# Column halves around the layer norms of a hybrid encoder step, and memory attention cut into steps

## What is computed

```python
x = LN1(ALPHA * x + 0.5 * swiglu1(x))                 # FFN width 2816
proj = x @ w_mix_in                                   # conv input, q, k, v, index queries and keys
x = LN2(ALPHA * x + concat(conv(proj), topk_attention(proj)) @ w_mix_out)
x = LN3(ALPHA * x + mem_attention(x @ w_mem_q, mem_k, mem_v) @ w_mem_o)   # 4 heads, 256 memory rows
x = LN4(ALPHA * x + 0.5 * swiglu2(x))
```

## Time and profile before

| | |
|---|---|
| three runs | 2760.41, 2766.08, 2769.19 us, median 2766.08 |
| profiled execution | span 2761.0 us from first to last instruction; no other time is given for it |
| TensorE matmuls | busy 2571.3 us (93% of the span), mean granted clock 0.946 |
| VectorE, ScalarE, GpSimd | busy 1042.4, 968.6, 1324.2 us |
| HBM | 218.93 MB read, 21.87 MB written |

### The profile page before, as it was taken

How to read it: one execution, slowest core, us unless ns; L and a number is a source line. 1 busy time by engine, 2 the same in 40 slices (tenths; PEclk the granted TensorE clock), 3 DMA queues, 4 the chain that set the end, 5 groups by cost and what they waited for, 6 DMA issues and landing times.

```text
span 2761.0 us, 40053 instructions
## 1 busy us (share of the span) xinstructions
PE 2571.3 (93%) x15097; PEld 2214.4 (80%) x15097; DVE 1042.4 (38%) x1705; ACT 968.6 (35%) x1469; POOL 1324.2 (48%) x717
## 2 busy tenths in 40 slices
PE   7899999898799998997989989999999899899997
PEld 6899999898688886774489789999965676688885
DVE  3000001605573004237562488888335625200003
ACT  4432323323333333326523333232345242433332
POOL 1366666533366667540024246666620332566665
PEclk9999999899899999997689989999989899899998
DMA  6422332234233332335022123322230222333332
GB/s 187 144 84 84 92 92 70 77 87 165 62 99 96 95 89 75 90 99 157 9 62 92 43 66 91 92 86 85 81 132 1 62 61 61 92 99 101 113 98 73
DMA packets 420706, 244.39 MB, mean 89 GB/s; under 512 B 23857, under 2 KB 412017, under 8 KB 419185
## 3 DMA queue, kind: packets, MB, share of 16 engines
q1 hardware_dynamic: 389088, 195.65, 24.5%
q10 hardware_dynamic: 27520, 23.34, 2.8%
q0 software_dynamic: 3984, 23.86, 2.4%
HBM read 218.93 MB, written 21.87 MB: 87 GB/s over the span
## 4 chain that ended last, share of the span: by engine, by line
PE 76%; DVE 6%; POOL 6%; issue 5%; ACT 4%; DMA 2%; ACTq 1%; POOLq 0%; DVEq 0%; SPq 0%
PE LIN L506 64%; PE LIN L673 4%; POOL WL L1519 3%; PE TR L687 2%; PE TR L701 2%; DVE Y L1292 1%; PE LIN L769 1%; DVE Y L1318 1%; PE LIN L740 1%; POOL HL L1596 1%; POOL FP L1593 1%; PE LIN L656 1%; PE LIN L612 1%; DVE QSUM L1236 1%; DMA WRAW<-in_w_mem_v 1%
## 5 line engine op out<-in xcount | busy, mean ns | idle before, releaser
L1519 POOL TENSOR_TENSOR WL<-WRAW,WH 128x1024 fp32r<-128x1024 f32 x366 | 882.9, 2413 | 826.5 <-ACT WH L806 805.5
L506 PE MATMUL LIN<-XH,WH 128*128 128x272 f32 (+2 forms) x3048 | 833.7, 328 | 42.7 <-DVE XL L1287 18.2
L506 PE MATMUL LIN<-XL,WH 128*128 128x272 f32 (+2 forms) x3048 | 829.7, 327 | 0.0
L506 PE MATMUL LIN<-XH,WL 128*128 128x272 f32 (+2 forms) x3048 | 825.6, 325 | 0.0
L506 PEld LDWEIGHTS LIN<-XH,WH 128*128 128x128 f32 (+1 forms) x3048 | 515.2, 191 | 98.3 <-issue 43.6
L506 PEld LDWEIGHTS LIN<-XL,WH 128*128 128x128 f32 (+1 forms) x3048 | 517.4, 191 | 45.1 <-issue 0.2
L506 PEld LDWEIGHTS LIN<-XH,WL 128*128 128x128 f32 (+1 forms) x3048 | 515.3, 190 | 46.0 <-issue 0.4
L806 ACT ACTIVATE WH<-WRAW 128x1024 fp32r<-128x1024 f32 x382 | 402.1, 1053 | 229.3 <-PE LIN L506 130.3
L811 ACT ACTIVATE FG<-LIN 128x512 f32<-128x512 f32 (+1 forms) x272 | 166.7, 613 | 845.5 <-PE LIN L506 843.5
L506 PE MATMUL LIN<-HH,WH 128*128 128x272 f32 (+2 forms) x1376 | 376.5, 323 | 9.4 <-DVEq L1503 3.8
L506 PE MATMUL LIN<-HL,WH 128*128 128x272 f32 (+2 forms) x1376 | 374.1, 321 | 0.0
(11 more groups left out here) (184 smaller groups left out, 1922.1 us busy)
## 6 DMA issues: line engine op xcount, KB each, us to landing
WRAW<-in_ffn_gate SPq DMA_DIRECT2D x88, 512.0 KB, 3.8
WRAW<-in_ffn_up SPq DMA_DIRECT2D x88, 512.0 KB, 3.8
WRAW<-in_ffn_down SPq DMA_DIRECT2D x64, 512.0 KB, 4.1
WRAW<-in_w_mix_in SPq DMA_DIRECT2D x44, 512.0 KB, 3.8
WRAW<-in_ffn_down SPq DMA_DIRECT2D x32, 384.0 KB, 3.4
WRAW<-in_w_mix_out SPq DMA_DIRECT2D x16, 512.0 KB, 4.2
WRAW<-in_w_mem_q SPq DMA_DIRECT2D x16, 512.0 KB, 4.2
WRAW<-in_w_mem_o SPq DMA_DIRECT2D x16, 512.0 KB, 4.1
```

The costliest lines, as they stand in the source:

```text
L506: last = pe.matmul(LIN[0:outputs, slot, a, 0:g.width], wt[:, w, c, 0:outputs], x[:, c, a * g.width:(a + 1) * g.width], start=(c == 0 and w ...
L1519: pool.tensor_tensor(WL[:, n % RING, :, :], WRAW[:, n % 2, :, :], WH[:, n % RING, :, :].bitcast(F32), ALU.subtract).then_inc(lo_split, 1)
```

## The change

- The sample rows move from group 0 to group 1, so group 0 has 512 columns and group 1 has 544. Each group has two halves of columns, 256 and 256, or 256 and 288.
- The stages and their loops give way to an unrolled plan. A run of stages of a group between two attentions is one segment without barriers ("chain").
- In mixout, memq, memo, the last down part of each FFN, and the first four tiles of mix and of FFN 2, products are made for a half: four weight tiles for half 0, then the same four for half 1. A tile is given back when half 1 has used it; then the tile four further on is split. Other products take all columns.
- A norm is cut into twelve steps for each half. Half 0's are hung on the last four half-1 products, half 1's on the first four half-0 products of what follows, each step in the middle ("mid") or at the end of a product. An engine does the mid steps of a product, then its own work for that product, then the weight split, then the end steps; TensorE does mid steps ahead of chunk 4.
- The shift by chunk 0's mean is now a matmul in the product itself (LESS1, and PART1 for chunk 0). CSUM is added by GpSimd for chunks 1 to 6. ALPHA is taken in with the product's addition; only ahead of FFN 2 ScalarE still scales, all eight chunks in step 11.
- Down products of the last part are added to Y by VectorE out of PSUM, without ScalarE and GpSimd. FFN_PARTS is 6, 8, 8, and a split takes only the chunks that a tile has.
- Memory attention is cut into four units (half, pair of heads) of seven steps, hung on memq's and memo's products. Its value products use a part of LIN of their own.
- The stores of conv rows of both groups come in the index stage of group 1. The final norm of group 1's tiles 0 and 1 is hung on the last half-1 products.

The core of the diff (in it, the last three pieces are VectorE's sums, VectorE's norm steps and GpSimd's loop):

```diff
-MEAN_AT, POWER_AT = 0, 8
-FFN_PARTS = [(0, 8), (8, 8), (16, 6)]
+MEAN_AT, POWER_AT = 288, 296
+FFN_PARTS = [(0, 6), (6, 8), (14, 8)]
...
-        self.sample = index == 0
+        self.sample = index == 1
...
+        self.halves = [(0, 256), (256, self.cols - 256)]
+        self.half_tiles = [[0, 1], [2, 3] + ([4] if self.sample else [])]
...
+        while k < len(tiles):
+            halves = blocks(k)
+            size = min(RING, len(tiles) - k) if halves else 1
+            for half in (0, 1) if halves else (None,):
+                for i in range(size):
+                    src, j, more = tiles[k + i]
+                    pr = self.add(base + k + i, name, j, g, half, nk, src[2])
+                    pr.tell(**facts, **more)
+                    made.append(pr)
+            k += size
...
+    last = [pr for pr in made if pr.half == 1][-4:]
+    for h, four in ((0, last), (1, [pr for pr in following if pr.half == 0][:4])):
+        def at(i, where, *steps):
+            (four[i].mid if where == "mid" else four[i].end).extend([("norm", norm, h, s) for s in steps])
+        at(0, "mid", 0)
+        if four[0].pair:
+            at(1, "mid", 1)
+        else:
+            at(0, "end", 1)
+        at(1, "end", 2, 3)
+        at(2, "mid", 4, 5)
+        at(2, "end", 6)
+        at(3, "mid", 7, 8)
+        at(3, "end", 9, 10)
+        if alpha:
+            at(3, "end", 11)
...
+    where = [(p, w) for p in memq[5:] + memo[:4] for w in ("mid", "end")][1:]
+    starts = {(0, 0): 0, (1, 0): 6, (0, 1): 13, (1, 1): 21}
+    for (h, q), at in starts.items():
+        for step in range(7):
+            pr, w = where[at + step]
+            (pr.mid if w == "mid" else pr.end).append(("memory", h, q, step))
...
+                for pr in prs:
+                    if pr.first:
+                        pe.wait_ge(lo_split, pr.tile + 1)
+                    if pr.turn:
+                        pe.wait_ge(product_read[pr.slot], pr.turn)
...
+                    if lead.kind == "down" and lead.j == 0:
+                        pe.wait_ge(hidden_lo, PLAN.hidden_done[lead.which, lead.g.index, lead.part, c, lead.half])
+                    if lead.after_norm is not None and lead.pair:
+                        low_wait(pe, lead.half, lead.after_norm, c)
...
+                        if c == pr.nk - 1:
+                            if pr.norm is not None and pr.j:
+                                out, col, w = pr.parts[0]
+                                pe.wait_ge(shift_source[pr.half], pr.norm + 1)
+                                last = pe.matmul(LIN[:, pr.slot, out:out + w], LESS1[:, :], XH[:, 0, col:col + w],
+                                                 start=False, stop=True)
...
+                if pr.norm is not None and pr.j == 1:
+                    pe.wait_ge(shift_source[pr.half], pr.norm + 1)
+                    pe.matmul(spread(pr.half, pr.w), PART1[:, :], XH[:, 0, cols(pr)], start=True, stop=True)\
+                        .then_inc(shift_done[pr.half], 1)
+                for strand in pr.mid:
+                    take_up(strand)
...
+                h, y = pr.half, Y[:, pr.j, cols(pr)]
+                dve.wait_ge(product, pr.p + 1)
+                if pr.name == "ffn":
+                    last = dve.tensor_tensor(y, in_psum(pr), y, ALU.add)
+                else:
+                    last = dve.scalar_tensor_tensor(y, y, ALPHA, in_psum(pr), ALU.mult, ALU.add)
+                last.then_inc(product_read[pr.slot], 1)
+                dve.wait_ge(product_read[pr.slot], pr.turn + 1)
+                if pr.j == 1:
+                    dve.wait_ge(shift_done[h], pr.norm + 1)
+                    dve.tensor_tensor(Y[:, 0, cols(pr)], Y[:, 0, cols(pr)], spread(h, pr.w), ALU.subtract)\
+                        .then_inc(first_centred[h], 1)
+                if pr.j == KD - 1:
+                    dve.wait_ge(chunk_added[h], (KD - 2) * (pr.norm + 1))
+                    dve.tensor_tensor(CSUM[:, cols(pr)], CSUM[:, cols(pr)], y, ALU.add).then_inc(sum_done[h], 1)
+                if pr.j >= 2:
+                    add_square(pr, pr.j - 1)
+                if pr.j == KD - 1:
+                    add_square(pr, pr.j)
...
+                if 3 <= step <= 10:
+                    j = step - 3
+                    if j == 0:
+                        dve.wait_ge(inv_done[h], norm + 1)
+                    y = Y[:, j, c0:c0 + w]
+                    dve.wait_ge(dve_step, less[h, j])
+                    done = after(dve.scalar_tensor_tensor(y, y, GCOL[:, gain_of(norm), j:j + 1], spread(h, w),
+                                                          ALU.mult, ALU.mult))
+                    if j + 4 < KD:
+                        less_mean(j + 4)
+                    dve.wait_ge(dve_step, done)
+                    dve.tensor_scalar(y, y, BCOL[:, gain_of(norm), j:j + 1], None, ALU.add).then_inc(biased[h], 1)
+                    if j - 1 in DVE_LOW:
+                        low_part(j - 1)
+                    if j == KD - 1:
+                        low_part(j)
...
+                elif name == "chain":
+                    for prs in paired(products):
+                        if prs[0].name == "ffn" and prs[0].which == 2 and not g.sample and prs[0].part == 1 \
+                                and prs[0].kind == "down" and prs[0].j == 0:
+                            reload_queries(GROUPS[1])
+                        for pr in prs:
+                            for strand in pr.mid:
+                                take_up(strand)
+                        for pr in prs:
+                            if pr.norm is not None:
+                                statistics(pr)
+                            elif pr.name == "ffn":
+                                consume_ffn(pr)
+                        for pr in prs:
+                            if pr.last:
+                                split_lo(pr.tile + RING)
+                        for pr in prs:
+                            for strand in pr.end:
+                                take_up(strand)
```

More of the change, by code:

```diff
@@ L202, in load_tiles, with __init__, tell @@
                      for col, rows in g.tiles]
-def half(i, m):
-    return i * 2 + m // 2
+class Product:
+    def __init__(self, p, tile, name, j, g, half, nk, rows):
+        self.p, self.tile, self.name, self.j, self.g, self.half = p, tile, name, j, g, half
+        self.nk, self.rows = nk, rows
+        self.slot = p % 2
+        self.turn = p // 2
+        self.col, self.w = (0, g.cols if g else N_MEM) if half is None else g.halves[half]
+        if half is None and self.w > 512:
+            self.parts = [(256, 0, 256), (512, 256, self.w - 256)]
+        else:
+            self.parts = [(0, self.col, self.w)]
+        self.first = self.last = False
+        self.pair = False
+        self.mid, self.end = [], []
+        self.event = 0
+        self.tell()
+    def tell(self, which=0, after_norm=None, norm=None, kind="", f=0, part=0):
+        self.which, self.after_norm, self.norm = which, after_norm, norm
+        self.kind, self.f, self.part = kind, f, part
@@ new lines, in memory_strands, with pair_up @@
+def memory_strands(memq, memo):
+    where = [(p, w) for p in memq[5:] + memo[:4] for w in ("mid", "end")][1:]
[4 more added lines that the diff above has]
+            (pr.mid if w == "mid" else pr.end).append(("memory", h, q, step))
+def pair_up(made):
+    for half in (0, 1):
+        two = [pr for pr in made if pr.half == half][:2]
+        for pr in two:
+            pr.pair = True
@@ L429, in mean_of, with paired, memory_parts @@
-        def mean_of(g, slot):
-            return TR[:, slot, :].rearrange("p (a b) -> p a b", a=2)[:, 0:g.parts, 0:g.width]
+                engine.wait_ge(x_lo[h], len(POOL_LOW) * norm + POOL_LOW.index(j) + 1)
+        def paired(products):
+            out, k = [], 0
+            while k < len(products):
+                n = 2 if products[k].pair else 1
+                out.append(products[k:k + n])
+                k += n
+            return out
+        def memory_parts(g, h):
+            return [(i, *g.tiles[t]) for i, t in enumerate(g.half_tiles[h])]
@@ L478, in begin @@
                     pe.wait_ge(pool_end, s)
-            def norm_before(s):
-                return STAGES[s - 1]["norm"] if s and STAGES[s - 1]["name"] == "ln" and STAGES[s - 1]["which"] != 4 \
-                    else None
-            def column_mean(g, slot, matrix, src):
-                for a in range(g.parts):
-                    last = pe.matmul(TR[:, slot, 512 * a:512 * a + g.width], matrix[:, :],
-                                     src[:, a * g.width:(a + 1) * g.width], start=True, stop=True)
-                return last
@@ new lines, in take_up, with prs_of_queries @@
+            def take_up(strand):
+                kind, *what = strand
+                if kind == "norm":
+                    norm_step(*what)
+                elif kind == "memory":
+                    memory_step(current[0], *what)
```

(21 more changed lines are left out.)

1826 lines of the change are left out of this document (924 added, 902 removed).

## The result

The changed kernel is slower: 2799.11 us median of 4 runs (2796.92 to 2804.11) against 2765.85 (2760.41 to 2769.19), a ratio of 1.0123 with a 95% interval of 1.0107 to 1.0139. The forecast was 2739 us, with a range up to 2790. Its profiled execution has a span of 2796.0 us, 35.0 more than before.

A forecast was written before the change was run, and what follows sets the result against it. A chain of waits, 76% TensorE, with time to win in breaks at norms and memory attention. Terms -24 - 4 + 3 + 3 - 3 - 2 = -27 took the 2761 us span to 2734, median 2739; own range 2725 to 2757, 8-in-10 range 2690 to 2790.

The forecast's parts named there:

- The step that failed: End of the kernel: group 1's top-k on VectorE still ends ahead of the final downs; no wait was priced.
- Norms: Six norms between product stages: steps stand beside half products, 107 us against 131.5, so -24 us.
- The lag of 7: In each norm, TensorE waits 7 us for VectorE's queued addition of the last half-1 product; bounds 2.5 and 10.5.
- Diagonals: In each norm, TensorE waits for SBUF-only diagonal operations at a product's end, once a half: 2.5 us (0 to 4).
- Memory attention: Both groups' memory attention: eight units beside products, 1 us of wait each, 84 us against 88: -4.
- FFN: Four FFNs: final downs wait 2 us more each, +8; less split work -4, one tile fewer -1: +3 (-2 to +8).
- 256-column halves: Group 0's 512-column products become two of 256, with starts at product ends: +3 us (0 to +6) in some 50 products.
- Load, index and attention: Load and index stages: conv-row stores move to the second index stage, ending waits for x_prompt: -3 us (-10 to +5).
- Tail: End of the kernel: three tiles remain of four, two move beside products: -2 us (-4 to +2).
- (b): Rival: VectorE's SBUF-only steps wait out splits at every half-1 end, 10.5 us a norm: 2787 us; chance 0.26 with above.
- (a): Rival: shared-port locks hardly bite, the six norms take 74 us: 2706 us; chance 0.23 with below.
- (c): Rival: TensorE waits as long in norms, VectorE's chain being as long: 2763 us, no difference; chance 0.14.

The follow-up runs named there:

- run 1: Changed kernel with group 0's last eight down products taken in whole by ScalarE and GpSimd: 2749.61 us, ratio 0.9952 to the kernel before.
- run 2: Changed kernel with group 1's top-k cut to 8 rounds a tile, leaving out part of the selection: 2751.82 us, ratio 0.9961 to the kernel before.
- run 4: Changed kernel with whole final downs in group 0, first three weight splits on GpSimd, twentieth split behind memkv's last copies: 2740.14 us, ratio 0.9916.
- run 10: Changed kernel with whole final downs in group 0 and the norm's bias addition on ScalarE, its start unchanged: 2717.25 us, ratio 0.9820.
- run 3: Changed kernel with the first three weight tiles split by GpSimd during the load instead of VectorE: 2797.40 us, ratio 1.0126 to the kernel before.
- run 6: run 4 with the four low parts beside each norm's last half-1 products cut to 16 of 128 columns: 2710.82 us, ratio 0.9812.
- run 5: run 4 with norm steps 7 and 8 moved behind VectorE's addition of the last half-1 product: 2725.59 us, ratio 0.9867.

## Why the prediction was wrong

**The step that failed** is the last sentence ahead of the sum: "VectorE's top-k of group 1 begins later, with the sample's beside it, and still ends ahead of the final downs". It measured 46.3 us of wait; runs 1 and 2 gave 49.5 and 47.3 back. The trace of before held all that was needed. VectorE's timeline of before, first and last operation of group 1's top-k:

```profile
1629.25 0.83 DVE L1195 MAX8 M<-SC 128x8 f32<-128x640 f32 x1 [0.30 <-issue]
...
1955.56 2.56 DVE L1199 TENSOR_SCALAR SC<-SC 128x1024 f32<-128x1024 f32 x1 [0.23 <-issue]
```

And TensorE's, the end of the last up product and the first matmuls of group 0's final downs:

```profile
1983.08 0.41 PE L506 MATMUL LIN<-XH,WL 128*128 128x272 f32 x2
1983.33 0.42 PE L506 MATMUL LIN<-HH,WH 128*128 128x272 f32 x2
```

The top-k took 329 us and ended at 1958.1; the final downs began at 1983.3, 354 us after its first operation: 25 us of cover. The change moved the sample's 17 passes, which take 1970.5 - 1937.8 = 32.7 us, into this top-k, and made the time that covers it shorter, by 43 us: some 26 are the sample's 32 columns, which left group 0 (a gate or up product takes 5.57 us, before 6.00), 10 are the parts of 6, 8, 8 tiles, with which less down work lies ahead of the final downs, and 7 are the top-k's later start (20.7 us after the FFN's first product, before 13.4). The final downs now began 311 us after the top-k's start. 364 us of top-k stood against 311 of cover. And the final downs had to wait for it only since their halves go to VectorE: before, its end was needed only by the next stage. I had written down that the halves' additions replace GpSimd's, as a saving, and not that they change queue.

**The term left out** is the start: 16.7 us in the profiles, 13 to 17 by all of them. I priced waits for weight splits at nothing and looked only at the ring's lead in the middle of the kernel, not at its filling, where VectorE's queue stands ahead of the first splits and the first copies behind the fourth tile's. Runs 4 and 10 bear it out in their times (9.5 and 10 to 14 us) and run 3 in its profile (8.5 us at the first FFN product), though not in its time.

**The terms that were priced** came to -42 us against -27 forecast, and what had no term to +13.5. That the sum of all this is again -28 is luck:
- Norms: -24 forecast, -31.8 measured. The lag of 7 (bounds 2.5 and 10.5) was 6.7 in norms 2 and 3, 6.0 in 4 and 5, 5.6 and 5.1 in 0 and 1. Its mechanism, too, holds: run 6, with narrow splits, took 23.5 of its 36.0 us away. Diagonals were in time, where I had put 2.5 us. Group 1's norms 1 and 4 gained only 1.6 and 0.6, the other four 6 to 8 each, depending on where the stretch is cut; why these two gained less stays open.
- Memory attention: -4 forecast, -14.4 measured. The window over it in group 0 shows TensorE with hardly a gap, at the full clock, so the wait of 1 us a unit never came:

```profile
1461.00:1541.00 80.00, 78.23 (x549) 74.12 (x550) 25.58 (x65) 32.92 (x83) 22.16 (x12) 1.00 0.19 54
```

- FFN: +3 forecast, +12.0 (9.8 and what the 46.3 leave of group 0's downs). TensorE's waits for HL are 9.0 us in 8 pieces, 1.8 the longest, in place of 2 us in four.
- 256-column halves: +3 forecast, +4.2. Load, index and attention: -3 forecast, -4.8. Tail: -2 forecast, -7.1. Projections and ends of stages, +13.5, had no term; what they are made of no run tells.

**The rivals.** (b) named 2787 and the right sign, with a price of 10.5 us a norm; the wait was 6.7 at most and norms became cheaper, so its mechanism is real but the slowdown wasn't its doing. (a) and (c) fall. The test I had named (a wait of 5 to 9 us between mixout and memq, bias additions over 1.5 us beside splits) came out right, and told nothing on the 46 us. Another sign did not: the norm windows were to be at a granted clock over 0.9, and the changed kernel's were at 0.79 to 0.87 (1578 to 1602: 0.79; 2203 to 2230: 0.87). Waits for WL, put at nothing, were small behind the start: 5.0 us in two.

## What to carry to other kernels

When a change hands work to another engine, look up what stands in that engine's queue at that time, in every place where the code runs, and compute both ends again: here the job in the queue got 35 us longer, the time that covered it 43 us shorter, and the 25 us between them went. When a sum comes out right, add up its terms one by one: two wrong ones can hide each other. Profile a stretch more than once before a difference of a few us in it is given a cause. Price the filling of a ring apart from its steady run. Where VectorE and GpSimd must work side by side, give the operations with all operands in SBUF to ScalarE first: in the changed kernel that was worth 37 us (32 of them in the norms), in the old one 8.

## What the runs showed of the hardware

- A VectorE bias addition on 256 columns takes 0.35 us, beside a GpSimd split of 2.4 up to 2.53; the same addition on ScalarE takes 0.49 to 0.54 beside the same splits, and VectorE operations that read PSUM keep 0.42.
- The same attention stage of group 1, with the same work, took 131.0 us at a granted clock of 0.89 in two versions (the changed kernel and run 1), 132.4 at 0.87 in run 5, and 134.8 to 135.2 at 0.85 or 0.86 in the nine others. Both kinds of start are among the slower ones (runs 2 and 10 with the changed start, runs 3, 4 and others with a mended one), so the start isn't the cause; what is stays open. Attention of group 0 took 86.5 us at 0.55 in run 10's profile, and 72.9 to 75.0 in all others. Such differences are as large as many effects looked for, so a part's gain is best read in its own stretch first.
